# Decoder step on one core: cache copies regrouped over two programs, output weights loaded in quarters

## What is computed

```
h     = rmsnorm(x) * (1 + sc1) + sh1                # sh, sc, ga from silu(c) @ w_ada
parts = split(h @ w_in)                             # mLSTM q,k,v,o,gates; 3 x (q,k,v); 2 merge gates
branch_a = mlstm_chunkwise(conv(parts[0]), ...) @ w_a
o_g, lse_g = dilated_window_attention(q_g, k_g, v_g, cache_g)     # windows 128, 512, 2048
branch_b = (softmax(lse) weighted sum of o_g) @ w_b
new_buf_g = concat(cache_g, new k,v)[:, -W_g:]      # the rolled caches are outputs
merged = sigmoid(parts[14]) * branch_a + sigmoid(parts[15]) * branch_b
x = x + ga1 * rmsnorm(merged @ w_out)
f = peer(rmsnorm(x)...)                             # 128 gathered experts per token
x = x + ga2 * rmsnorm(f)
```

## Time and profile before

| | |
|---|---|
| median of 3 runs | 2476.38 us (2470.22 to 2491.16) |
| profiled execution, first to last instruction | 2477.6 us, 1.2 above the median |
| PE / DVE / ACT / POOL busy | 87% / 50% / 30% / 30% of the span |
| DMA moved | 875.53 MB |

### The profile page before, as it was taken

The page is one execution under the profiler, slowest core; times in us unless marked ns, Lnnn a source line. Parts: engine busy times, 40 slices in busy tenths (PEclk is TensorE's granted clock), DMA queues, the critical chain, the costliest instruction groups (busy, mean ns, idle before and its releaser), DMA issues.

```text
span 2477.6 us, 25280 instructions
## 1 busy us (share of the span) xinstructions
PE 2143.7 (87%) x9074; PEld 1240.3 (50%) x9074; DVE 1232.3 (50%) x3183; ACT 754.7 (30%) x2192; POOL 733.9 (30%) x694
## 2 busy tenths in 40 slices
PE   6999989788898979999997888788879787878786
PEld 3777448666787655555553443343334333433221
DVE  1000001235233256555656866767676767676764
ACT  2010012231322034444243443343333333333322
POOL 0000001110102024434343444343544343545341
PEclk8999999898999989999999889898989898989899
DMA  8566649987886469999999999999999999999997
GB/s 358 208 238 266 256 161 372 328 289 307 304 315 220 160 265 398 386 399 405 387 386 399 419 391 394 416 419 411 420 419 413 420 418 409 406 420 419 421 419 293
DMA packets 125625, 875.53 MB, mean 353 GB/s; under 512 B 16080, under 2 KB 17392, under 8 KB 40636
## 3 DMA queue, kind: packets, MB, share of 16 engines
q0 software_dynamic: 85760, 691.32, 69.6%
q1 hardware_dynamic: 38788, 182.48, 19.4%
q10 hardware_dynamic: 952, 0.13, 0.0%
HBM read 861.54 MB, written 99.37 MB: 388 GB/s over the span
## 4 chain that ended last, share of the span: by engine, by line
PE 36%; DVE 14%; DMA 11%; ACT 2%; issue 2%; POOL 0%; ACTq 0%; POOLq 0%; DVEq 0%
PE ps L1947 25%; DMA pr_ring<-in_uv,pr_idx 11%; PE ps L1843 3%; DVE pr_ring L2169 3%; PE ps L1883 3%; PE ps L1892 1%; PE ps L1905 1%; PE ps L1865 1%; DVE pr_hot L2149 1%; DVE pr_hot L2153 1%; DVE pr_ind L2130 1%; DVE pr_ind L2127 1%; DVE pr_pick L2156 1%; ACT pr_coef L2019 1%; DVE pr_val L2129 1%
## 5 line engine op out<-in xcount | busy, mean ns | idle before, releaser
L1947 PE MATMUL ps<-pr_ring,pr_diag 128*128 128x512 f32 (+1 forms) x2224 | 1045.5, 624 | 208.6 <-ACT pr_diag L2023 208.6
L1828 POOL DMA_INDIRECT pr_ring<-in_uv,pr_idx x556 | 638.9, 1149 | 960.2 <-PE ps L1947 818.6
L2169 DVE CUSTOM_DVE_ANT_0 pr_ring<-pr_ring,h 128x1024 f32<-128x1024 f32 x556 | 662.8, 1223 | 357.3 <-DMA pr_ring<-in_uv,pr_idx 356.0
L1947 PEld LDWEIGHTS ps<-pr_ring,pr_diag 128*128 128x128 f32 (+1 forms) x2224 | 425.2, 195 | 773.8 <-issue 475.5
L2014 ACT ACTIVATE pr_gel<-pr_dots 128x2 f32<-128x2 f32 x288 | 58.0, 201 | 522.0 <-DVE pr_dots L2169 521.4
L2023 ACT ACTIVATE pr_diag<-ident,pr_coef 128x128 f32<-128x128 f32 x512 | 173.6, 386 | 0.0
L2019 ACT ACTIVATE pr_coef<-pr_gel,pr_wgt 128x1 f32<-128x1 f32 x576 | 138.3, 287 | 27.0 <-ACT pr_gel L2014 0.4
L1843 PE MATMUL ps<-trunk,pr_wq 128*128 128x320 f32 (+2 forms) x544 | 132.1, 397 | 3.0 <-ACT trunk L2049 2.2
L474 PE MATMUL ps<-trunk,ap_ring 128*128 128x288 f32 x384 | 126.3, 411 | 2.9 <-PEq L192 2.9
L475 PE MATMUL ps<-trunk,ap_ring 128*128 128x288 f32 x384 | 125.2, 408 | 0.0
L1843 PEld LDWEIGHTS ps<-trunk,pr_wq 128*128 128x128 f32 x544 | 100.3, 194 | 41.9 <-issue 15.1
(11 more groups left out here) (320 smaller groups left out, 2273.5 us busy)
## 6 DMA issues: line engine op xcount, KB each, us to landing
out_win_s<-in_cache POOLq DMA_DIRECT2D x64, 1020.0 KB, 8.1
side_unit<-in_w_merge SPq DMA_DIRECT2D x32, 768.0 KB, 8.0
sa_ring<-in_cache SPq DMA_DIRECT2D x24, 1024.0 KB, 10.0
late_ring<-in_w_ada SPq DMA_DIRECT2D x8, 2048.0 KB, 17.3
sa_ring<-in_kcacheB SPq DMA_DIRECT2D x16, 1024.0 KB, 8.4
pr_wq<-in_peer_wq SPq DMA_DIRECT2D x16, 1024.0 KB, 8.9
out_win_s<-in_cache POOLq DMA_DIRECT2D x16, 1008.0 KB, 13.3
ap_ring<-in_w_attn_qk SPq DMA_DIRECT2D x6, 2048.0 KB, 20.5
```

The lines of the kernel that those rows point to most:

```text
L1828: pool.indirect_dma_start(row(n), None, d["uv"], bass.IndirectOffsetOnAxis(ap=idx[:, b % 4, j:j + 1], axis=0)).then_inc(arrived[slot(n)], 16)
L1947: mm = pe.matmul(ps[0:r, bank + half, :], diag[:, slot(n), 0:r], row(n)[:, o:o + CHUNK], start=h == 0 and j == 0, stop=b == FINAL[i] and j ...
L2169: ins = dve.tensor_tensor_reduce(u, u, e.h2[:, BLOCKS[b][0], :], 1.0, 0.0, ALU.mult, ALU.add, dots[:, slot(n):slot(n) + 1])
```

## The change

The cache copies are written as 128 rows instead of 16. In `project`, POOL issues one copy after each even unit and two after each odd one, for all units but the last three: 54 copies instead of 39. In `prompt_attention` it issues two at even steps and three at odd ones until the list is empty: 34 copies, the last two at step 13 of 0 to 15. In `mlstm_and_merge`, load 11 comes before `w_out`, `w_out` is cut into four quarters of 1 MB, and loads 12 and 13 come behind the second and the fourth; the state stores follow them. `product(i)` waits for both quarters of a half.

```diff
@@ roll_pieces
-                out.append((d[f"win{g}_s"][s, at:at + size].rearrange("(a n) -> a n", a=16),
-                            d[f"cache{g}"][s, LS * D + at:LS * D + at + size].rearrange("(a n) -> a n", a=16)))
+                out.append((d[f"win{g}_s"][s, at:at + size].rearrange("(a n) -> a n", a=P),
+                            d[f"cache{g}"][s, LS * D + at:LS * D + at + size].rearrange("(a n) -> a n", a=P)))
@@ project, gpsimd
-                for u in range(len(units)):
-                    if k.rolls:
-                        pool.wait_ge(s_mm, u + 1)
+                for u in range(len(units) - 3):
+                    pool.wait_ge(s_mm, u + 1)
+                    for _ in range(1 + u % 2):
                         dst, src = k.rolls.pop()
                         pool.dma_start(dst, src).then_inc(k.s_roll, 16)
@@ prompt_attention, gpsimd
-                    for _ in range(min(3 if s else 4, len(k.rolls))):
+                    for _ in range(min(3 if s % 2 else 2, len(k.rolls))):
@@ mlstm_and_merge, sync
                 sp.wait_ge(sa.s_used, 2 * NS * sa.PARTS)
-                for n in range(2):
-                    sp.dma_start(o.w[:, n], d["w_out"][n]).then_inc(o.s_w[n], 16)
+                mg.load(sp, TAIL + 2)
+                for q in range(4):
+                    n, half = divmod(q, 2)
+                    cs = slice(half * KD // 2, (half + 1) * KD // 2)
+                    sp.dma_start(o.w[:, n, cs, :], d["w_out"][n][:, cs, :]).then_inc(o.s_w[n], 16)
+                    if q % 2:
+                        mg.load(sp, TAIL + 3 + n)
                 sp.wait_ge(s_c, PT)
...
-                for t in range(TAIL, mg.UNITS - 2):
+                for t in range(TAIL + 3, mg.UNITS - 2):
                     mg.load(sp, t + 2)
@@ output_and_experts, tensor
-                            pe.wait_ge(front.s_w[n], 16)
+                            pe.wait_ge(front.s_w[n], 32)
```

## The result

The changed kernel takes 2454.91 us (median of 11 runs, 2445.06 to 2463.45) against 2476.38 (11 runs, 2458.84 to 2491.16). The ratio is 0.9912, with a 95% interval of 0.9888 to 0.9935: faster by 21 us, or 0.9%, where 34 us were forecast. It lies inside the range of 2434 to 2462, but above the forecast's own 2434 to 2450 (chance 0.60) and in rival A's 2452 to 2465 (0.20). It is just under the 1% that the forecast gave 0.66 to.

What follows compares the result with a forecast made beforehand. DMA bounds the expert gather from 1300 us; PE's gaps set the rest. 5.5 + 2.9 + 1.7 + 1.3 + 13.3 + 2.6 + 6.8 + 2.9 - 3 = 34.0 us off 2476.4 gave 2442; range 2434 to 2450.

Steps and rivals of the forecast that it cites:

- rival A: Projections: copies hold up the late chunks, costing 12 us instead of 3, plus clock falls; 2455 us, chance 0.20.
- 1, rows: Cache copies: as built, each keeps the same 16 rows on both sides, so nothing is gained.
- 2, ends of programs: Two program ends: with no copy near them, POOL's drain stops holding PE; gain 5.5 and 2.9 us.
- 3, the clock behind them: PE's matmuls after the two program ends: shorter gaps keep the clock at 2.4 GHz; gain 1.7 and 1.3 us.
- 4, attention: Attention: five fewer copies by step 6 bring load 4 sooner, gain 13.3 us, plus 2.6 for the clock.
- 5, merge: Merge: load 11 ahead of `w_out` removes PE's wait, gain 6.8 us, plus 2.9 for the clock.
- 6, projections: `project`: more copies beside the late chunks may make them late; loss 3 us, taken between 0 and 12.
- Rival B: Attention: the wait for load 4 only shrinks, 8.9 us gained instead of 13.3, no clock gain; 2449 us, chance 0.12.
- Rival C: Projections: DMA carries less with two copies in POOL's queue, costing 52 us; 2491 us, chance 0.08.
- Rival D: Whole change: it does not do what it says; held true for the rows, not the order; no chance given.

Runs made afterwards that it cites:

- strided twin with 64 KB: The changed kernel with each copy taking strided rows that the build cannot join, 16 rows of 64 KB a copy; 2461.4 us in one run.
- late chunk first: The changed kernel with SP issuing the late chunk ahead of the job's weights in the attention projections; 2441.47 us, ratio 0.9863.
- real rows: The changed kernel with copies of the two large caches cut into 128 strided rows of 8 KB that the build cannot join; 2440.52 us, ratio 0.986.
- the ends of the programs: The kernel before, without copies after the last three projection units and in the last two attention steps, leftovers issued earlier in the attention; 2478.2 us in one run.
- the run of this part alone: The kernel before with only the new order of merge loads and output weights; 2463.26 us, ratio 0.9961.

## Why the prediction came out as it did

Its steps, against what the traces show:

- **1, rows: nothing.** Right: the shape as built is the same. The changed kernel and its strided twin with 64 KB agree within 0.3 us in the late landing and in the projections.
- **2, ends of programs: 5.5 and 2.9.** Measured 5.7 (7.59 to 1.87) and 2.95 (4.35 to 1.40). Right for the first end by its own experiment. For the second the reason was only half: there it is not the last copy but how many are still queued; the run with 28 copies by step 6 had none in the last two steps and waited 11.8. One detail of the forecast was wrong: POOL's drain did not fall under 1 us. It runs 9.8 us from 343.1, longer than before, but nobody waits for it. At the second end it runs 2.8 us from 521.0, though the last copies had landed by 508.6, so a drain is not all copies. The first end:

```profile
L427 POOLq DRAIN  x1: 9849/9849/9849, 343.1 to 343.1; - x1
...
L427 ACTq DRAIN  x1: 8/8/8, 361.3 to 361.3; - x1
```

- **3, the clock behind them: 1.7 and 1.3.** Nothing in the profile of the changed kernel. The two places of the earlier trace rows, after:

```profile
361.55 0.91 PE L663 MATMUL ps<-a_qk 128*128 128x128 f32 x6 [1.87 <-PEq L427]
363.76 1.65 PE L663 MATMUL ps<-a_qk 128*128 128x128 f32 x6 [1.30 <-DVE pa_nb L703]
366.55 9.68 PE L584 MATMUL ps<-trunk,mp_ring 128*128 128x288 f32 x32 [1.14 <-DMA mp_ring<-in_w_mlstm]
```

```profile
531.08 2.79 PE L835 MATMUL ps<-trunk,sa_spread 128*32 128x384 f32 x16 [2.06 <-POOL sa_spread L797]
```

PE starts at full clock, 6 matmuls in 0.91 us, and has the lower level two us later, and the 32 matmuls take 9.68 us as before. But this is one execution. Nine of the profiles of this study have the short idle of 1.87 us before the attention, and in three of them (late chunk first, real rows, the ends of the programs) the clock held and the 32 matmuls took 8.03. In the last of these three:

```profile
348.66 0.91 PE L663 MATMUL ps<-a_qk 128*128 128x128 f32 x6 [1.87 <-PEq L427]
350.87 0.94 PE L663 MATMUL ps<-a_qk 128*128 128x128 f32 x6 [1.31 <-DVE pa_nb L703]
353.27 8.03 PE L584 MATMUL ps<-trunk,mp_ring 128*128 128x288 f32 x32 [1.46 <-DMA mp_ring<-in_w_mlstm]
```

The small products and the idle between them are the same or longer there, so these alone do not decide it, and what does is not shown. In the three profiles with 7.5 to 8.0 us of idle PE was at the lower level from the start, 1.62 us for the 6 matmuls. At the second end line 835 ran at the lower level in all twelve profiles, for at least most of its 2.54 to 2.79 us. So the step booked as certain what three of nine profiles show at the first end and none at the second.

- **4, attention: 13.3 + 2.6.** The wait went wholly, 14.5 + 2.6, and with the second end this is the stage's 20.0 us. The size was not what the working gave: five copies are 13.3 us of DMA time, but load 4 landed 13.9 us after its issue instead of 39.2, 25.3 sooner, since the stores ahead of it were gone too. The working also counts load 3 among SP's own 4.2 MB ahead of load 4; it had landed at 413.9, before load 4's issue, so 3.1 MB at most stood there. PE at step 6, after:

```profile
444.90 0.82 PE L677 MATMUL ps<-ident,pa_prob 128*128 128x128 f32 x6
445.55 3.62 PE L587 MATMUL ps<-mp_ring,trunk 128*128 128x256 f32 x16
```

- **5, merge: 6.8 + 2.9.** Measured 10.4 by the stage, 9.3 in the run of this part alone. Load 11 landed after 4.1 us, 4.9 were taken. Nothing over 0.5 us took its place; products 11 and 12 start without a wait:

```profile
781.80 1.98 PE L1447 MATMUL ps<-ml_vm,ml_kw 64*128 64x512 f32 x4
783.71 3.72 PE L1254 MATMUL ps<-trunk,side_unit 128*128 128x256 f32 x16
...
791.00 3.72 PE L1254 MATMUL ps<-trunk,side_unit 128*128 128x256 f32 x16
```

- **6, projections: 3 lost. This is the step that failed in size.** It cost 12.1 us (312.3 against 300.2 with the late chunk first). The bound from above, all five copies ahead of the chunk, gave 22.6 to 23.9 us of landing and 12 us of loss; the chunks landed after 22.9 to 24.4 and, in the token job, 27.2. I had taken a quarter of that bound because the copies had kept to their part before the change. Five copies, the chunk and its job's weights are 9.4 MB, in 22.8 us 413 GB/s, and the DMA moved 402 there: they use up all of it. The place was right:

```profile
280.65 3.64 PE L369 MATMUL ps<-late_ring,silu_c 128*32 128x128 f32 x64 [7.00 <-DMA late_ring<-in_w_ada]
```

The token job's chunk, with a slack of 20.1 us, costs 7.0 us and another 1.7 for the clock behind it (3.64 against 1.95), most of the whole loss. It landed later than the 23.9 of the bound: it was still in flight when POOL issued a sixth copy, at 273.94. That the bound's 12 us agree with the 12.1 is in part luck: it had at most 3.8 for this chunk, where 8.7 were lost, and 8 for the others, which lost 3.4.

Rival A (the copies hold up the late chunks, 2455 us) named this mechanism, and its time was met. Its sum does not give it, though: 12 us and four times 1.7 are 18.8, not the 16 that it took off, and the time from that is 2458. Against such a sum 6.7 us less were lost in the projections and 2.2 more gained in steps 2, 4 and 5, while the 3 of step 3 did not come and the last stage took 2.9 more. That the time of 2455 was met to 0.1 us is luck. Rival B (the wait for load 4 only shrinks) is refuted by the absent wait. Rival C (the DMA carries less) too: it moved 402 GB/s where the forecast had 394. Rival D was true for the rows and only for them.

Measured by stages: 5.7 + 2.95 + 17.1 + 10.4 - 12.1 = 24.1, and PE is 24.2 us earlier at line 1870. Of the 10 us that this is under the forecast, 9.1 are step 6 and 3.0 step 3; the others gave 2.2 more. The last stage, 2.9 us longer by scatter, makes 21 of it.

## What to carry to other kernels

When transfers share a full DMA, sort each queue by the time at which its data are needed: one swap of two lines, the urgent chunk ahead of weights with two jobs of slack, was worth 12 us, and moving background copies out of the chunk's flight was worth as much. A wait that goes may only move: before promising its time, ask whether the stage as a whole is bounded by DMA; here curing the middle brought 20 us of idle at the end, and it took less traffic in the stage, and less of it early, to shorten it. Look at the shape that was built, not the one that was written. And when the traces show a full resource and counting bytes gives a bound, do not book a quarter of it without a reason that a trace shows.

## What the runs showed of the hardware that was not expected

How a memory-to-memory copy is cut into rows changes how much other queues get beside it: with rows of 64, 32 and 8 KB the same 2 MB chunk behind 2 MB of weights landed after 23.0, 21.5 and 15.8 us. A drain on POOL lasts until its copies have gone, however many are queued: 9.8, 16.5 and 23.6 us in three runs, each over some 2 us after its last copy landed, and it holds all engines if it is the last. And after an idle of 1.9 us PE still ran at 2.4 GHz in all nine profiles that have it (6 matmuls in 0.91 to 0.95 us), but within the small, broken work behind it fell to 1.2 GHz in six of them and not in three; behind the idles of 4.2 us or more at these two ends it started at 1.2 GHz.
